# The last two token tiles of the output projections as two groups of one tile

## What is computed

```
out_l = mixed @ w_out                  # layer 0: K = 1024, layer 1: K = 2048; N = 1024
x     = layer_norm(alpha * x + gate * out_l, ln_g, ln_b)
```

## Time and profile before

| | us |
|---|---|
| median of three runs | 3270.16 |
| the profiled execution, its own time | 3269.38 |
| its span, first to last instruction | 3267.6 |
| layer 0, last matmul of the output projection to the last normalization | 1705.22 to 1719.46 |
| layer 1, the same | 3248.67 to 3262.91 |

### The profile page before, as it was taken

One profiled execution on the slowest core, in us unless ns is written; L12 is line 12 of the kernel. 1 busy time (PEld: TensorE's weight loads), 2 busy tenths in 40 slices (PEclk: granted clock), 3 DMA queues, 4 the chain that ended last, 5 costly groups with the idle time before them and its releaser, 6 DMA issues. The chain is left out here.

```text
span 3267.6 us, 48116 instructions
## 1 busy us (share of the span) xinstructions
PE 2596.7 (79%) x19846; PEld 2212.9 (68%) x19846; DVE 1657.3 (51%) x2457; ACT 918.9 (28%) x1443; POOL 849.3 (26%) x778
## 2 busy tenths in 40 slices
PE   4899999846888753556675989989688989899687
PEld 2577667746777642455564767768588989899575
DVE  2037886533464435887375435435544444444333
ACT  1114323311223214443303222222233333332211
POOL 1211111044655602555222111111011111111322
PEclk8899999977989876778897989999899999999898
DMA  6512554533333213010432233232411212110521
GB/s 249 209 59 82 161 166 136 162 102 80 91 108 77 78 47 81 16 41 33 147 125 62 98 85 100 100 110 71 161 62 72 85 72 85 72 53 1 199 97 58
DMA packets 286368, 317.86 MB, mean 97 GB/s; under 512 B 112083, under 2 KB 233374, under 8 KB 283478
## 3 DMA queue, kind: packets, MB, share of 16 engines
q1 hardware_dynamic: 261152, 314.41, 29.7%
q10 hardware_dynamic: 25014, 0.60, 0.4%
HBM read 202.31 MB, written 112.56 MB: 96 GB/s over the span
## 5 line engine op out<-in xcount | busy, mean ns | idle before, releaser
L2684 PE MATMUL PS<-Q,K 128*128 128x128 f32 x2560 | 302.7, 281 | 62.8 <-DMA Q<-q_d 53.9
L2684 PEld LDWEIGHTS PS<-Q,K 128*128 128x128 f32 x2560 | 298.9, 198 | 65.8 <-DMA Q<-q_d 55.1
L2802 POOL TENSOR_TENSOR weights_lo<-weights,weights_hi 128x1664 fp32r<-128x1664 f32 x32 | 121.4, 3793 | 600.0 <-ACT weights_hi L2760 600.0
L2711 PE MATMUL PS<-V_hi,weights_hi 128*128 128x258 f32 x832 | 238.3, 286 | 5.3 <-DVE H L2910 2.7
L375 PE MATMUL PS<-hT_hi,w_in_hi 128*128 128x512 f32 (+1 forms) x640 | 242.4, 379 | 0.0
L377 PE MATMUL PS<-hT_hi,w_in_lo 128*128 128x512 f32 (+1 forms) x640 | 238.8, 373 | 0.0
L376 PE MATMUL PS<-hT_lo,w_in_hi 128*128 128x512 f32 (+1 forms) x640 | 238.8, 373 | 0.0
L2712 PE MATMUL PS<-V_lo,weights_hi 128*128 128x258 f32 x832 | 235.3, 283 | 0.0
L2713 PE MATMUL PS<-V_hi,weights_lo 128*128 128x258 f32 x832 | 234.5, 282 | 0.0
L375 PE MATMUL PS<-h_hi,w_in_hi 128*128 128x512 f32 (+1 forms) x624 | 228.2, 366 | 5.2 <-PEq L109 5.2
L376 PE MATMUL PS<-h_lo,w_in_hi 128*128 128x512 f32 (+1 forms) x624 | 224.6, 360 | 0.0
(11 more groups left out here) (379 smaller groups left out, 5932.8 us busy)
## 6 DMA issues: line engine op xcount, KB each, us to landing
chunk_in<-in_d SPq DMA_DIRECT2D x40, 512.0 KB, 3.4
w_in<-in_e_w_in_dram SPq DMA_DIRECT2D x30, 512.0 KB, 5.0
xnew<-in_o_w_in_dram SPq DMA_DIRECT2D x30, 512.0 KB, 5.3
in_d<-xnat SPq DMA_DIRECT2D x20, 640.0 KB, 6.2
modw<-in_mod_w_dram SPq DMA_DIRECT2D x8, 1536.0 KB, 19.3
xnat<-in_mod_w_dram SPq DMA_DIRECT2D x8, 1536.0 KB, 7.3
v_d<-xnew SPq DMA_DIRECT2D x16, 640.0 KB, 3.0
k_d<-xc SPq DMA_DIRECT2D x16, 640.0 KB, 2.9
```

The lines of the kernel that those rows point to most:

```text
L2684: last = pe.matmul(PS[:, 4 + x % 4, (j - j0) * P:(j - j0 + 1) * P], K[:, kt, j * P:(j + 1) * P], Q[:, kt, i * P:(i + 1) * P], start=(kt == ...
L2711: pe.matmul(out, wh, VH[:, j, q], start=(j == seen[0]), stop=False)
```

## The change

```diff
-OUT_GROUPS = [(4, 4, 2), (4, 2, 2)]
+OUT_GROUPS = [(4, 4, 1, 1), (4, 2, 1, 1)]
 YRING = 3
```

## The result

The changed kernel takes 3285.99 us (median of 18 runs, 3278.14 to 3290.24) against 3270.86 for the kernel before in the same rounds. The ratio is 1.0042, with a 95% interval of 1.0034 to 1.0049. Forecast were 3284 us and a ratio of 1.0043.

A forecast was written before the change was run, and what follows sets the result against it. TensorE was taken to bound quiet steps, late norms' square roots to hold the others, with VectorE tails exposed. Layer 0's +8.7 and layer 1's +5.5 us on 3269.38 give 3283.6; the median's 0.8 makes 3284 us, range 3274 to 3296.

The forecast's parts named there:

- The tail: VectorE's work after each layer's last matmul: one take and one norm fewer, 14.2 us down to 7.17.
- Slice 5 behind the store: Last groups: slice 5's load waits behind the late tile's store, ready at S + 12.0, wanted at S + 6.8.
- Where the group before ends (S): Start of each layer's last group, at the previous group's last matmul: 1703.4 in layer 0, 3232.7 in layer 1.
- Clock: Slow-clock costs: 1.2 GHz for layer 0's slices 6 and 7, 1.0 us in layer 1, 1.5 per last group.
- The 1.0 us in layer 1's third group: Loss over the ten steps remaining in layer 1's last group but one, for a clock that came back late.
- The 1.5 us for each last group: Clock loss after the gap ahead of slice 5 in each layer's last group, bounds 0 and 3.0 us.
- The sum: Both output projections together: +8.7 us in layer 0 and +5.5 in layer 1, +14.2 in all.
- The low part beside a norm: GpSimd's low part of 128 columns while VectorE normalizes: 1.46 us, bounds 0.46 and 1.73.
- a norm's period: VectorE's time per norm beside steps of one tile: 6.01 us instead of 6.28.
- the clock didn't stay low in the quiet steps: Rival: layer 1's single groups run at 1.2 GHz to their end, +39 us, 3310 us; chance 0.08.
- the ring: Rival: three load buffers bound the one-tile steps, +6.5 us over layer 1's 21 quiet steps, 3291 us; chance 0.10.
- the last group was held by the late norm: Opposite of the not-slower rival: slice 5 is there in time, only +1.5 us, 3272 us; chance 0.08.

The follow-up runs named there:

- the store's other place: Changed kernel with the late tile's store after all loads of y in each layer's last group: 3274.92 us against 3271.50 for the kernel before.
- the first experiment: Single groups in one layer only, against the kernel before (3271.50 us): layer 1 alone 3276.97 us, layer 0 alone 3277.89 us.

## Why the prediction was right, point by point

- **The tail**: 7.17 us forecast, 7.3 measured. The gain was real, 6.9 us a layer, and was more than spent. The last matmul comes 14.5 us later in layer 0 and 12.8 in layer 1, counted from the takes above; 15.8 and 12.5 were forecast.
- **Slice 5 behind the store**: ready at S + 12.0 by the forecast, at S + 11.8 in both layers (1710.05 to 1721.85, 3245.49 to 3257.24). Confirmed by the store's other place. Two terms in it were off and cancelled: the loads behind the store landed 1.9 to 2.6 us after their issue and not 3.4, and the late tile was normalized at S + 7.8 in layer 0 and S + 7.7 in layer 1 and not at S + 7.2. That the point came out within 0.2 us is in part luck.
- **Where the group before ends (S)**: layer 0 32.7 us after the take of its second group by the forecast, 32.9 measured; layer 1 33.75 and 32.8.
- **Clock**: of the four terms one held. Slices 6 and 7 of layer 0's third group went at 1.2 GHz, as I took it (matmuls 0.43 us apart from 1704.40 to 1709.38). The 1.0 us in layer 1's third group was hardly there: its last ten steps took 13.9 us (3231.58 to 3245.49) instead of 13.6, and 0.3 us of that kind also stands in layer 0's last three slices at 2.4 GHz. The 1.5 us for each last group was wrong in both layers, with opposite signs: layer 0 had none (three slices in 4.4 us), layer 1 2.7 (18.0 us for 11 slices of 1.36, less the same 0.3). So 0 and nearly the 3.0 of my bounds were reached, behind gaps of 3.3 and 3.4 us. The kernel before has more of these: the 3.30 us ahead of 1686.94 and the 3.29 ahead of 3168.77 were followed by matmuls 0.43 us apart at once, the 3.28 ahead of 3156.22 by matmuls 0.23 apart, which fell to 0.43 only 1.2 us later. The length of such a gap doesn't tell here which level follows.
- **The sum**: layer 0 7.6 instead of 8.7, layer 1 5.8 instead of 5.5, together 13.4 instead of 14.2, or 11.8 with the longer stretches of layer 0 from the first experiment. The medians say 15.1. The mechanism was right; that the forecast of 13.8 for the medians lies within 1.3 us of it owes something to terms that were off in both directions, the clock's above all.
- **The low part beside a norm** was mis-sized: 1.46 forecast, 0.45 measured for the slice right behind a square root (the next slice's, where it fell beside L2200, took 1.25 and 1.32), and a norm's period 6.21 us instead of 6.01 (see the last section). The slices come 1.0 us sooner, and the norms between them 0.2 later each.
- **Rivals**: the clock didn't stay low in the quiet steps (1.00 from 3264.00), the ring isn't the bound (steps of 1.36 us; loads there landed in 1.8 to 2.1 us), and the last group was held by the late norm.
- **The chances**: 0.56 stood on no change beyond 0.5%, and the measured 0.42% lies there. But I had written that under 0.5% can't be told from no change, and that was wrong: 18 runs of each tell 0.42% from zero plainly, with an interval of 0.34 to 0.49% slower. "Within 0.5%" was a band and not a finding of no effect.

## What to carry to other kernels

When work of one stage is tucked among the steps of the next by fixed positions in an instruction stream, those positions are in steps, and their meaning in us changes when the steps get shorter: a store that stood between two loads and held no matmul up (in layer 1's last group of the kernel before TensorE's only gap is the 3.15 us, behind a square root) holds the whole pipeline once a step lasts 1.36 us instead of 2.72. So before splitting work to shorten a tail, compute when each wait in each queue is fulfilled (here S + 7.2 by the forecast, S + 7.7 in the trace) and which step needs what is queued behind it (here S + 6.8). And look at the idle time that the kernel already has in such places: the same kind of misplaced waits cost 22.6 us in the kernel before by the medians, 25.1 by the traces, more than the 14.1 that the split could ever bring.

## What the runs showed that I had not expected

VectorE and GpSimd beside each other: with 256 columns GpSimd's low part beside a norm took 1.73 us instead of 0.74, and L2200 was lengthened. With 128 columns it is the other way for the slice right behind a square root. The timelines of both engines after, around one square root:

```profile
1691.37 0.45 POOL L2108 TENSOR_TENSOR y_in_lo<-y_in,y_in_hi 128x128 fp32r<-128x128 f32 x1 [5.76 <-ACT y_in_hi L2227]
...
1691.34 1.57 DVE L2199 SCALAR_TENSOR_TENSOR resid<-resid,mean_var,ln_row 128x1024 f32<-128x1024 f32 x1
1692.94 1.28 DVE L2200 SCALAR_TENSOR_TENSOR xnew<-resid,rstd,ln_row 128x1024 f32<-128x1024 f32 x1
```

The low part takes 0.45 us, as if alone; L2199, which starts 0.03 us ahead of it in the trace, takes 1.57 us instead of 1.28. The smaller slice's high part ends 0.11 us sooner, and that seems to be enough for GpSimd to come first, although the trace shows VectorE's instruction starting first by a hair. The Trainium skill (SBUF — State Buffer, "SBUF: two separate sides") has it that the one that starts first holds the shared port pair and the other blocks; who is first can't be read off starts that are 0.03 us apart. That this is the cause was not tested. Where the order can be read, the trace agrees with the rule: the low part of the slice after the last late norm started 0.35 us behind L2200 and took 1.25 us instead of 0.45.

```profile
1705.37 1.28 DVE L2200 SCALAR_TENSOR_TENSOR xnew<-resid,rstd,ln_row 128x1024 f32<-128x1024 f32 x1
...
1705.72 1.25 POOL L2108 TENSOR_TENSOR y_in_lo<-y_in,y_in_hi 128x128 fp32r<-128x128 f32 x1 [1.47 <-ACT y_in_hi L2227]
```
